# First feed-forward matmul with the weight blocks stationary and 256 tokens moving

## What is computed

```python
u = x * (1.0 + sc2) + sh2
ff = jnp.square(jax.nn.relu(u @ w_ff1[l])) @ w_ff2[l]
x = _layer_norm(DEEPNORM_ALPHA * x + (1.0 + g2) * ff, ln2_g[l], ln2_b[l])
```

## Time and profile before

| | value |
|---|---|
| median of 3 runs | 2442.67 us |
| lowest and highest | 2441.25, 2450.8 us |
| span of the profiled execution, first to last instruction | 2440.1 us |
| TensorE (PE) busy | 2296.8 us, 94% |
| VectorE (DVE) busy | 1717.9 us, 70% |
| ScalarE (ACT) busy | 1115.2 us, 46% |
| mean granted TensorE clock | 0.974 |
| mean DMA rate | 254 GB/s |

### The profile page before, as it was taken

The page is one execution under the profiler, slowest core; times in us unless marked ns, Lnnn a source line. Parts: engine busy times, 40 slices in busy tenths (PEclk is TensorE's granted clock), DMA queues, the critical chain, the costliest instruction groups (busy, mean ns, idle before and its releaser), DMA issues.

```text
span 2440.1 us, 31697 instructions
## 1 busy us (share of the span) xinstructions
PE 2296.8 (94%) x10608; PEld 1911.6 (78%) x10608; DVE 1717.9 (70%) x1891; ACT 1115.2 (46%) x1390; POOL 203.1 (8%) x388
## 2 busy tenths in 40 slices
PE   3689999989999999999989999998999999999996
PEld 2578887868878878888878888877888888888885
DVE  6888788967666666676878878888645455454566
ACT  2235543355435435445444554434653543543542
POOL 2211111100000000000100111110000000000000
PEclk9789999989999999999989999998999999999998
DMA  9977888948887887886966888896556556556563
GB/s 354 382 278 288 306 303 312 348 160 274 274 281 253 279 292 241 278 287 234 342 241 214 287 285 294 309 327 225 176 188 195 184 189 194 187 188 193 173 223 109
DMA packets 174099, 619.10 MB, mean 254 GB/s; under 512 B 19600, under 2 KB 20368, under 8 KB 173968
## 3 DMA queue, kind: packets, MB, share of 16 engines
q1 hardware_dynamic: 114064, 407.50, 48.2%
q0 software_dynamic: 55296, 201.35, 23.7%
q10 hardware_dynamic: 4608, 8.39, 1.1%
HBM read 615.07 MB, written 2.10 MB: 253 GB/s over the span
## 4 chain that ended last, share of the span: by engine, by line
PE 82%; DVE 10%; issue 3%; ACT 2%; DMA 2%; ACTq 0%; SPq 0%; DVEq 0%; POOLq 0%
PE bank L1124 26%; PE bank L1126 25%; PE bank L1125 25%; DVE mod_acc L677 4%; PE bank L1169 2%; PE bank L1149 2%; DVE w_lo L662 1%; ACT w_hi L379 1%; ACT utmp L396 1%; DMA raw<-w_out_dram 1%; PE bank L1160 1%; DVE xt L765 1%; DMA Z<-w_mod_dram 0%; DVE xt L768 0%; DMA lnc<-ln_cols_dram 0%
## 5 line engine op out<-in xcount | busy, mean ns | idle before, releaser
L662 DVE TENSOR_TENSOR w_lo<-raw,w_hi 128x1024 fp32r<-128x1024 f32 x768 | 938.2, 1224 | 635.9 <-ACT w_hi L379 633.9
L379 ACT ACTIVATE w_hi<-raw 128x1024 fp32r<-128x1024 f32 x768 | 812.6, 1060 | 1161.1 <-PE bank L1126 1050.6
L1124 PE MATMUL bank<-w_hi,u_hi 128*128 128x512 f32 x1792 | 718.4, 401 | 11.2 <-DVE u_lo L703 5.7
L1126 PE MATMUL bank<-w_lo,u_hi 128*128 128x512 f32 x1792 | 705.6, 394 | 0.0
L1125 PE MATMUL bank<-w_hi,u_lo 128*128 128x512 f32 x1792 | 704.7, 393 | 0.0
L1124 PE MATMUL bank<-w_hi,m_hi 128*128 128x512 f32 x1280 | 501.5, 392 | 3.2 <-DVE m_lo L703 3.2
L1126 PE MATMUL bank<-w_lo,m_hi 128*128 128x512 f32 x1280 | 499.4, 390 | 0.0
L1125 PE MATMUL bank<-w_hi,m_lo 128*128 128x512 f32 x1280 | 499.1, 390 | 0.0
L1124 PEld LDWEIGHTS bank<-w_hi,u_hi 128*128 128x128 f32 x1792 | 341.8, 191 | 81.8 <-DVE u_lo L703 7.3
L1126 PEld LDWEIGHTS bank<-w_lo,u_hi 128*128 128x128 f32 x1792 | 340.6, 190 | 73.3
L1125 PEld LDWEIGHTS bank<-w_hi,u_lo 128*128 128x128 f32 x1792 | 341.8, 191 | 68.7
(11 more groups left out here) (107 smaller groups left out, 944.9 us busy)
## 6 DMA issues: line engine op xcount, KB each, us to landing
raw<-w_ff_dram SPq DMA_DIRECT2D x512, 512.0 KB, 4.0
mod_raw<-w_mod_dram POOLq DMA_DIRECT2D x320, 512.0 KB, 5.8
raw<-w_in_dram SPq DMA_DIRECT2D x192, 512.0 KB, 5.5
Z<-w_mod_dram POOLq DMA_DIRECT2D x64, 512.0 KB, 8.8
raw<-w_out_dram SPq DMA_DIRECT2D x64, 512.0 KB, 6.7
Z<-ln_g_dram ACTq DMA_DIRECT2D x16, 256.0 KB, 7.0
Z<-ln_b_dram ACTq DMA_DIRECT2D x16, 256.0 KB, 8.8
xt<-x_dram SPq DMA_DIRECT2D x4, 512.0 KB, 11.7
```

What stands on the lines that cost most here:

```text
L379: nc.scalar.activation(w_hi[:, j % AHEAD, :], raw[:, j % RAW, :], ACT.Copy).then_inc(hi_ready, 1)
L662: nc.vector.tensor_tensor(w_lo[:, j % AHEAD, :], raw[:, j % RAW, :], w_hi[:, j % AHEAD, :].bitcast(F32), ALU.subtract).then_inc(lo_ready, 1)
L1124: nc.tensor.matmul(o, hi[:, k, tok], wh, start=(k == 0), stop=False)
L1126: ins = nc.tensor.matmul(o, hi[:, k, tok], wl, start=False, stop=(k == KC - 1))
```

## The change

A new function `up_group` takes the place of `group` in the up units. The weight block (128 inputs by 128 hidden channels) is now stationary and all 256 tokens move. Per block of 128 inputs there are 4 such channel blocks, each with three matmuls of 256 columns, so a group has 24 matmuls of 256 columns. The result has channels on partitions, with two channel blocks side by side in a bank.

`relu_square` now reads the banks into `utmp`, squares there, and copies both halves to `m_hi` at once, at the end of the up unit. `hid`, `hidden` on ScalarE and `turn_hidden` on TensorE are gone, and with them their share of the bank schedule (`LOOP_H`, the "loop" and "last h" jobs). `split_low` for the hidden values stands one group earlier on VectorE (j == 1 where it was j == 2).

```diff
-            def relu_square(b, u0):
+            def relu_square(b, u0, layer, block_no, s):
                 par = u0 % 2
+                n = SPLITS * layer + 24 + 8 * block_no + 2 * s
                 act.wait_ge(pair_used, at(b, 64, 8 * u0 + 8))
-                for t in range(T):
-                    ins = nc.scalar.activation(hid[:, t, :], pacc[par][t][:], ACT.Relu)
+                act.wait_ge(split_ready, at(b, 8, n))
+                for i in range(2):
+                    ins = nc.scalar.activation(utmp[:, i, :], pacc[par][i][:], ACT.Relu)
                 ins.then_inc(acc_read[par], 1)
                 act.wait_ge(acc_read[par], at(b, 4, u0 // 2 + 1))
-                nc.scalar.activation(hid[:], hid[:], ACT.Square).then_inc(hid_ready, 1)
+                nc.scalar.activation(utmp[:], utmp[:], ACT.Square).then_inc(hid_ready, 1)
+                act.wait_ge(hid_ready, at(b, 4, 4 * (BLOCKS * layer + block_no) + s + 1))
+                for i in range(2):
+                    chunk = 4 * s + 2 * i
+                    nc.scalar.activation(m_hi[:, chunk:chunk + 2, :], utmp[:, i, :], ACT.Copy).then_inc(split_hi, 1)
...
-            def hidden(layer, b, s, block_no, job0):
...
-                            if v < 4 and j == 2:
-                                hidden(layer, b, v, 0, JOB[("loop", layer)] + LOOP_H[v])
                         if v in (0, 1, 2, 7):
-                            relu_square(b, base + 1 + v)
+                            relu_square(b, base + 1 + v, layer, int(v == 7), (v + 1) % 8)
...
-                            if v < 4 and j == 2:
+                            if v < 4 and j == 1:
                                 for i in range(2):
                                     n = b * 8 + (SPLITS * layer + 24 + 2 * v + i)
                                     split_low(n, utmp_pair(i), m_hi, m_lo, 4 * v + 2 * i)
...
+            def up_group(label, slot, k0, acc_pair):
+                pe.wait_ge(lo_ready, label + 1)
+                for kk in range(GK):
+                    k = k0 + kk
+                    for c in range(4):
+                        o = acc_pair[c // 2][:, c % 2 * SEQ:(c % 2 + 1) * SEQ]
+                        wh = w_hi[:, slot, kk * NCOL + c * P:kk * NCOL + (c + 1) * P]
+                        wl = w_lo[:, slot, kk * NCOL + c * P:kk * NCOL + (c + 1) * P]
+                        nc.tensor.matmul(o, wh, u_hi[:, k, :], start=(k == 0 and c % 2 == 0), stop=False)
+                        nc.tensor.matmul(o, wh, u_lo[:, k, :], start=False, stop=False)
+                        ins = nc.tensor.matmul(o, wl, u_hi[:, k, :], start=False, stop=(k == KC - 1 and c % 2 == 1))
+                ins.then_inc(pair_used, 1)
...
-                def turn_hidden(unit_index, job, bank=None, reads=None):
-                    pe.wait_ge(hid_ready, unit_index)
-                    for i in range(2):
-                        turn(job + i, lambda c, t: hid[:, t, (2 * i + c) * P:(2 * i + c + 1) * P],
...
```

More of the change, by code:

```diff
@@ L141, in transpose_jobs @@
         add(("fill", 2 * layer + 1), 8)
-        add(("loop", layer), 3 * (8 + 2 * modded))
-        add(("last h0", layer), 2)
+        add(("loop", layer), 3 * 2 * modded)
         add(("last gate", layer), 4)
-        add(("last h1", layer), 6)
         if modded:
@@ L632, in mlp @@
                     if v < 3:
-                        relu_square(None, last + v)
+                        relu_square(None, last + v, layer, BLOCKS - 1, v + 1)
             act.wait_ge(small_in, 16 * 9)
@@ L999, in mlp @@
                 modded = layer < DEPTH - 1
[L1000 removed]
+                stride = 2 * modded
                 q0 = (layer * MOD_LAYER + MIX_SLABS) * KC
@@ L1138, in unit_groups @@
                         pe.wait_ge(split_ready, operand + (j + 1))
-                    group(8 * unit + j, j % AHEAD, GK * j, pacc[par], hi, lo)
+                    if up:
+                        up_group(8 * unit + j, j % AHEAD, GK * j, pacc[par])
+                    else:
+                        group(8 * unit + j, j % AHEAD, GK * j, pacc[par], hi, lo)
                     if side is not None:
@@ L1209, in both @@
                     side(j)
-                unit_groups(None, unit, u_hi, u_lo, operand=fill // 2 * SPLITS + fill % 2 * 16, side=both)
+                unit_groups(None, unit, u_hi, u_lo, operand=fill // 2 * SPLITS + fill % 2 * 16, side=both,
+                            up=fill % 2 == 1)
             def mixer(layer):
@@ L1344, in side @@
                         def side(j, v=v):
[L1345 to L1348, removed]
                             if modded and (v, j) in ((4, 1), (7, 7)):
-                                off = 8 + (v == 7)
+                                off = int(v == 7)
                                 reduce_slab(int(v == 7), b * stride + (loop0 + off), bank=(loop0 + off) % 2,
@@ L1356, in mlp @@
                         unit_groups(b, base + 1 + v, u_hi if up else m_hi, u_lo if up else m_lo,
-                                    operand=b * 8 + split0 if v == 3 else None, side=side)
+                                    operand=b * 8 + split0 if v == 3 else None, side=side, up=up)
                 last = base + 8 * (BLOCKS - 1) + 1
@@ L1360, in side @@
                     def side(j, v=v):
-                        if v < 4 and j == 2:
-                            turn_hidden(16 * layer + 4 * (BLOCKS - 1) + v + 1,
-                                        JOB[("last h0", layer)] if v == 0 else JOB[("last h1", layer)] + 2 * (v - 1))
                         if v == 0 and j == 5:
                             gate_rows(6 * layer + 5, JOB[("last gate", layer)],
-                                      loop0 + 9 if modded else JOB[("red", layer, 5)])
+                                      loop0 + 1 if modded else JOB[("red", layer, 5)])
                         if modded and (v, j) == (4, 1):
@@ L1371, in mlp @@
                     unit_groups(None, last + v, u_hi if v < 3 else m_hi, u_lo if v < 3 else m_lo,
-                                operand=split0 + 8 * (BLOCKS - 1) if v == 3 else None, side=side)
+                                operand=split0 + 8 * (BLOCKS - 1) if v == 3 else None, side=side, up=v < 3)
                 if modded:
```

21 lines of the change are left out of this document (4 added, 17 removed).

## The result

The changed kernel takes 2455.72 us (median of 8 runs, 2451.01 to 2462.81) beside 2446.31 for the kernel before in the same session: a ratio of 1.0044, 95% interval 1.0033 to 1.0055, some 9.4 us slower. The prediction said 2420. Its profiled execution has a span of 2449.3 us, 9.2 above that of before; it is the fastest of the eight runs (2451.01).

The account below looks back on a forecast made before the run. TensorE, busy for 94% of the span, was taken as the bound. Turns -29.1, matmuls 0 and jumps +6 gave -23 us, so 2442.67 - 23 = 2420 us; 8-in-10 range 2407 to 2464.

Parts of the forecast that it names:

- Part 2: Up units' matmuls: 3072 of 512 columns become 6144 of 256; claimed 0 us, bounds -10 and +72.
- g: Step of one 256-column fp32r matmul in the up units: taken as 0.1133 us, bounds 0.1117 and 0.125.
- B: Rival for the up units' matmuls: all extra is per matmul, g = 0.120, sum +18, 2461 us; chance 0.25.
- A: The forecast case: up-unit matmuls' extra goes by column, 2420 us, own range 2409 to 2430; chance 0.45.
- the float32 rows: Trace steps of float32 matmuls, 128 and 256 columns: a part of 0.005 us claimed not to grow with columns.
- rival C: Up units' weight load no longer hidden beside the stream: g = 0.125, sum +49, 2492 us; chance 0.10.
- Part 1: Turns (transposes) after the up units go: 32 x 0.91 = 29.1 us saved, nothing hiding them.
- Part 3: TensorE's jumps back: shorter queued matmuls cover less, about 3 us each at layer 1's two; +6 us, bounds 0 and +13.
- n: Number of matmuls queued on TensorE that run on during a jump back: claimed near 20.
- My equation: For TensorE's jumps back: 0.227 n + 0.3 = 0.11 n + 2.67, giving a jump of about 4.9 us.
- Part 4: ScalarE and VectorE: moved copies and added waits fit in 3.9 us of room before TensorE needs weights; counted 0.
- rival D: Something else, such as late weights from unit-end copies, takes the turns' place: 29.1 us return, 2449 us; chance 0.04.

Follow-up runs that it names:

- e9: Kernel before with five TensorE loops of 64 or 256 matmuls appended, other engines done: no open stretch at any of 15 jumps; 0.120 us a step at 256 fp32r columns.
- e4: Kernel before, tokens stationary and turns kept, each 512-column matmul of the up units cut into two of 256: 2483.46 us, ratio 1.0153.
- e1: Kernel before with series of single-width matmuls appended: fp32r steps 0.227, 0.174, 0.120, 0.1115, 0.1115 us at 512, 384, 256, 192, 128 columns.
- e7: Kernel before with fp32r series appended: alternating 512/256 pairs take 0.354 us; 320, 288 and 224 columns take 0.1465, 0.1315 and 0.1115 us.

## Why the prediction was wrong

**Part 2 failed, at one term: g.** "I take per column, 0.1133" is refuted. The step is 0.120 in the kernel, on an idle core (`e9`), and with the roles as before (`e4`): all of the 0.0133 is per matmul. The term is +40.9 us, not 0, and it alone turns a forecast of 23 us faster into a slower kernel. That 2455.7 lies inside the range of 2407 to 2464 is owed to the part of B that this range took in; A's own ended at 2430. Rival B named the mechanism and its price, and gave 2461; I ranked it below A on an argument from the float32 rows, whose 0.005 extra I used to say that the rest must go by column. These rows could not carry it. The 128-column one is at the load's own 0.1117, so its 0.005 over the stream is the floor of the load and no extra at all, and `e1` shows the same 0.1115 for fp32r of 192 and 128 columns. (The other row, float32 of 256 columns with 0.22 over 0.213, no run went after.) Without that reason the trace left per matmul and per column level, and a chance of 0.45 against 0.25 was more than it gave. The rule of the Trainium skill that I quoted spoke for B: its size was wrong for fp32r, its kind was right.

The bounds were right: 0.1117 is the step below 256 columns (`e1`, `e7`), and rival C is excluded, since load and stream of nearly equal length do lie side by side.

**Part 1 was right.** 22.65 to 21.79 in a down unit that held a turn, and 23.90 to 23.04 in an up unit between `e4`, which has narrow matmuls and turns, and the changed kernel: 0.86 a turn by both, where 0.91 was expected; over 32 turns that is 1.6 us.

**Part 3 was near in layer 1's trace, by a mechanism with a condition missing, and does not show in the medians.** 2.65 and 2.4 us open per jump, +4.9 in all against +6; no half clock behind them, which I had allowed for (in `e4` it followed one jump of two, so that is partly luck). By the medians, with loops and without, the change made the jumps no dearer (0, with some 5 either way). Loops of their own give n = 30 and a jump of 5.0 us, the kernel itself 24 and 5.5, where I had 20 and 4.9. My equation was loose: it put n short matmuls ahead of layer 0's jump, where the row has 16. With 16 x 0.11 + 2.67 = 4.4 us for the jump n is 18, so the term hardly moves.
**Part 4 was right.** In the changed kernel's waits no wait on ScalarE's copies appears behind up units; rival D did not happen. With its g corrected the sum is -29.1 + 40.9 + 6 = +18, 2461; the kernel measured +9.4 in the same session. In the trace the terms close in layer 1's feed-forward part (+10.6 against 10.8), and what is missing lies in the mixers, where it comes with the run, and in layer 0's feed-forward part (+1.5 against 5.9), where it stays unexplained. A few us of this kernel's time are not read from any one profiled execution.

## What to carry to other kernels

Count instructions as well as columns: halving the width of an fp32r matmul at unchanged work adds 0.0133 us for each one more, and at 256 columns that is 12% of its stream. Before trading transposes for narrower matmuls, put 24 of the new shape behind a kernel and read the step; that run would have decided this case. A floor of another kind (here the load's) in a neighbouring row must not be read as an extra of the kind in question.

## What the runs showed that I had not expected

- fp32r: 0.0133 us fixed a matmul at 512, 384, 320 and 256 columns (0.0115 at 288); bf16: 0.0025. Alternating 512 and 256 columns adds 0.007 a pair.
- A 128 x 128 four-byte load takes 0.1115 us, and no fp32r matmul with a load of its own comes faster, at 224, 192 or 128 columns.
- A jump back on TensorE is free with a body of 768 matmuls and their loads, and takes about 5 us from 832 on, of which 24 to 30 queued matmuls (an estimate) cover their own time. Up to 768 the second round loads no instructions, from 832 on it loads them all again. Jumps of ScalarE and VectorE over the same blocks cost nothing that shows in the time.
